# Experts four at a time in column tiles of 32 slots, with plain fp32 weights, and dilated sums on VectorE

## The reference

```
q = rms_norm_2(heads(q, DIL_DH), dil_q_norm_g[l, gi])
k = rms_norm_2(heads(k, DIL_DH), dil_k_norm_g[l, gi])
...
def hier_moe(h, w_rg, b_rg, w_re, b_re, w_gate, w_up, w_down):
    g_sel = jnp.argmax(g_logit, axis=-1)                 # one group of experts per token
    top_v, top_i = lax.top_k(e_logit, TOP_K)             # two experts in it
    gate = jax.nn.softmax(top_v, axis=-1) * g_p[:, None]
    ...
    def expert_block(args):
        xb, e = args
        return (jax.nn.silu(xb @ w_gate[e]) * (xb @ w_up[e])) @ w_down[e]
    ...
    out = jnp.zeros((T + 1, D), jnp.float32).at[row_t].add(yb.astype(jnp.float32) * row_w[:, None])[:T]
```

## Time and profile before

| | us |
|---|---|
| median of 3 runs | 3622.94 |
| lowest, highest | 3620.98, 3625.41 |
| the profiled execution | 3620.94 |
| its span (first to last instruction) | 3619.1 |
| experts' first product | 3025.05 |
| end of the experts' products | 3603.19 |

### The profile page before, as it was taken

How to read it: one execution, slowest core, us unless ns; L and a number is a source line. 1 busy time by engine, 2 the same in 40 slices (tenths; PEclk the granted TensorE clock), 3 DMA queues, 4 the chain that set the end, 5 groups by cost and what they waited for, 6 DMA issues and landing times. The chain is left out here.

```text
span 3619.1 us, 45453 instructions
## 1 busy us (share of the span) xinstructions
PE 3464.6 (96%) x17876; PEld 2860.6 (79%) x17876; DVE 2210.6 (61%) x3051; ACT 1413.9 (39%) x1566; POOL 413.2 (11%) x327
## 2 busy tenths in 40 slices
PE   7999999998999999999979999999998998999998
PEld 6888888755978887888749888977877877888886
DVE  7746547548755468567877333653226336999998
ACT  4211111447422232222335222433324225877876
POOL 2000000200110012000322000100000012333331
PEclk9999999999999999999989999999999998999999
DMA  6423323210244335444342222231222226999997
GB/s 252 136 84 117 104 91 105 74 50 1 94 137 142 110 112 180 146 160 154 97 123 76 93 94 85 73 133 59 82 93 70 88 90 240 364 362 361 366 377 296
DMA packets 321395, 531.12 MB, mean 147 GB/s; under 512 B 20564, under 2 KB 276609, under 8 KB 295360
## 3 DMA queue, kind: packets, MB, share of 16 engines
q1 hardware_dynamic: 307872, 512.46, 40.8%
q0 software_dynamic: 11040, 12.91, 1.1%
q10 hardware_dynamic: 2304, 3.24, 0.4%
HBM read 519.91 MB, written 25.17 MB: 151 GB/s over the span
## 5 line engine op out<-in xcount | busy, mean ns | idle before, releaser
L552 PE MATMUL banks<-operand_hi,trunk_weights_hi 128*128 128x512 f32 (+1 forms) x1568 | 566.8, 362 | 28.1 <-DVE trunk_weights_lo L1347 11.4
L552 PE MATMUL banks<-operand_lo,trunk_weights_hi 128*128 128x512 f32 (+1 forms) x1568 | 558.7, 356 | 0.0
L552 PE MATMUL banks<-operand_hi,trunk_weights_lo 128*128 128x512 f32 (+1 forms) x1568 | 558.5, 356 | 0.0
L552 PEld LDWEIGHTS banks<-operand_hi,trunk_weights_hi 128*128 128x128 f32 x1568 | 298.6, 190 | 78.7 <-DVE trunk_weights_lo L1347 13.1
L552 PEld LDWEIGHTS banks<-operand_lo,trunk_weights_hi 128*128 128x128 f32 x1568 | 298.8, 191 | 41.7
L552 PEld LDWEIGHTS banks<-operand_hi,trunk_weights_lo 128*128 128x128 f32 x1568 | 298.1, 190 | 42.1
L4390 DVE TENSOR_TENSOR ex_w_lo<-weight_ring,ex_w_hi 128x2048 fp32r<-128x2048 f32 x128 | 291.7, 2293 | 41.3 <-ACT ex_w_hi L4318 41.3
L1347 DVE TENSOR_TENSOR trunk_weights_lo<-weight_ring,trunk_weights_hi 128x2048 fp32r<-128x2048 f32 x90 | 206.0, 2288 | 163.1 <-ACT trunk_weights_hi L1302 163.1
L4318 ACT ACTIVATE ex_w_hi<-weight_ring 128x2048 fp32r<-128x2048 f32 x128 | 245.4, 1918 | 76.6 <-PE banks L4216 63.5
L1302 ACT ACTIVATE trunk_weights_hi<-weight_ring 128x2048 fp32r<-128x2048 f32 x90 | 171.7, 1908 | 215.8 <-PE banks L552 215.5
L552 PE MATMUL banks<-trunk_hidden_hi,trunk_weights_hi 128*128 128x512 f32 (+1 forms) x672 | 233.1, 347 | 4.1 <-DVE X L1373 1.7
(11 more groups left out here) (615 smaller groups left out, 7270.5 us busy)
## 6 DMA issues: line engine op xcount, KB each, us to landing
weight_ring<-ffn_w SPq DMA_DIRECT2D x120, 1024.0 KB, 4.9
weight_ring<-w_mod SPq DMA_DIRECT2D x72, 1024.0 KB, 4.9
weight_ring<-w_gate SPq DMA_DIRECT2D x64, 1024.0 KB, 7.4
weight_ring<-w_up SPq DMA_DIRECT2D x64, 1024.0 KB, 7.1
room<-w_down SPq DMA_DIRECT2D x64, 1024.0 KB, 7.1
weight_ring<-w_in SPq DMA_DIRECT2D x26, 1024.0 KB, 5.0
weight_ring<-ffn_w SPq DMA_DIRECT2D x16, 768.0 KB, 4.4
weight_ring<-o_w_pw SPq DMA_DIRECT2D x8, 1024.0 KB, 6.7
```

Source lines behind the costliest of these rows:

```text
L552: ins = pe.matmul(bank[:, at:at + width], w, x[:, at:at + width], start=start and n == 0, stop=stop and n == len(passes) - 1)
```

## The change

Three things change.

First, the experts are taken four at a time (a quad; the loop's step for one quad is a unit). The 128 columns of PE's array are four tiles of 32: tile j holds 32 slots of expert j of the quad, and `side_by_side` (L4424) issues for the four tiles a plain fp32 product each. There are three sets of 32 slots, so a round holds 96 slots of each expert. A unit has 6 phases (gate, up, down, two each); in each, four chunks, one of each expert, are used by all three sets. The weights are not split: PE reads the landed chunks. There are 16 places of 1 MB (2 + 4 + 8 + 2 in `expert_room`, the weight ring and `room`), and all of the first 16 chunks are loaded during `project_and_route`. The chunks of a phase are replaced when it is done (`load_after`): experts 0 and 1 of the quad by SP, 2 and 3 by ACT between its activations. The last unit's rows are multiplied by their gates, split into high and low, and brought to their tokens by fp32r products; the additions of the chosen rows are written beside the last phases.

Second, the router cuts the places into 18 blocks of 32 slots instead of 4 of 128, adds each expert's first lane, and has no entries for the last expert's gates.

Third, the squares of the dilated query heads are turned and summed in blocks of 32 by DVE (L3529, L3530), and one `fold` of four products (L3539) at the end of the stage adds the four blocks for all heads.

```diff
-            if dst is dil["q"]:
-                def pe_part(pe, bank, s):
-                    pe.wait_ge(s.act, s.acts_before(projected - 1))
-                    for t in range(ST):
-                        at = 512 + (g * GH + m) * ST + t
-                        ins = pe.matmul(k.PS[3][:, at:at + 1], sq(i)[:, t // 2, (t % 2) * P:(t % 2 + 1) * P], k.ones[:, 0:1], start=True, stop=True)
-                    return ins
+        def squares_summed(i, head):
+            def dve_part(dve, bank, s):
+                if head:
+                    dve.wait_ge(s.dve, s.dves_before(projected[i]) - 1)
+                for u in range(2):
+                    s.link(dve, dve.transpose(turned, sq(i)[:, u, :]))
+                    ins = dve.tensor_reduce(partial[:, head, 2 * u:2 * u + 2, :], turned.rearrange("p (t b c) -> p t b c", t=2, c=BLOCK), AXX, ALU.add)
...
+        def fold(pe, bank, s):
+            pe.wait_ge(s.dve, s.dves_before(queries[-1]))
+            for b in range(P // BLOCK):
+                ins = pe.matmul(k.PS[3][b * BLOCK:(b + 1) * BLOCK, 512:512 + GROUPS * GH * ST].rearrange("p (h t) -> p h t", t=ST),
+                                k.fold[:], partial[:, :, :, b], start=True, stop=True)
...
             def split_off(act, bank, s):
-                if i >= 2:
+                if i - 2 in summed:
                     act.wait_ge(s.out, summed[i - 2] + 1)
+                elif i >= 2:
+                    act.wait_ge(s.dve, s.dves_before(projected[i - 2]))
...
-CHUNKS = 6
+QUADS, QUAD, SETS, ROUNDS = EXPERTS // 4, 4, 3, 6
+PHASES, ROOM = 6, 16
+CHUNKS = PHASES * QUAD
...
-            sp.wait_ge(s_wlo, SLOTS + PIECES - 1)
-            for c in (*GATE, *UP):
-                load_expert_chunk(k, sp, c, 0, other=int(c in UP))
+            for c in range(2):
+                load_expert_chunk(k, sp, 0, c, 0)
+            for c in range(SLOTS):
+                sp.wait_ge(s_wlo, c + PIECES)
+                load_expert_chunk(k, sp, 0, 2 + c, 0)
+            sp.wait_ge(s_out, KD)
+            for c in range(6, 10):
+                load_expert_chunk(k, sp, 0, c, 0)
             for t in range(ST):
                 sp.wait_ge(s_ca, 2 * t + 2)
                 sp.dma_start(k.rows_dram[t * P:(t + 1) * P, :], HR[:, t, :]).then_inc(s_rows, 16)
+            for c in range(10, ROOM):
+                load_expert_chunk(k, sp, 0, c, 0)
...
+        def load_after(eng, p, u, f, which):
+            phase_done(eng, p, u, f)
+            for j in which:
+                if f < 2:
+                    load_expert_chunk(k, eng, u, QUAD * (f + 4) + j, 8 * (p % 4) + 4 * u)
...
-            def three(out, x, w, start, stop):
-                passes = ((x[0], w[0]), (x[0], w[1]), (x[1], w[0]))
-                for i, (a, b) in enumerate(passes):
-                    ins = pe.matmul(out, a, b, start=start and i == 0, stop=stop and i == 2)
-                return ins
+            def side_by_side(out, s, x, f, u, at, start, stop):
+                for j in range(QUAD):
+                    lanes = slice(BLOCK * j, BLOCK * (j + 1))
+                    ins = pe.matmul(out[lanes], x[:, lanes], raw[(CHUNKS * u + QUAD * f + j) % ROOM][:, at:at + 512], start=start, stop=stop)
+                return ins
+            def phase(f, s, p, u):
+                if s == 0:
+                    for j in range(QUAD):
+                        n = CHUNKS * u + QUAD * f + j
+                        pe.wait_ge(landed[n % ROOM], 48 * p + 16 * (n // ROOM + 1))
+                if f < 4:
+                    for i in range(4):
+                        kk = 4 * (f % 2) + i
+                        ins = side_by_side(G(s) if f < 2 else U(s), s, XT[:, s, kk, :], f, u, 512 * i, kk == 0, kk == KD - 1)
...
+            for i in range(6):
+                if i >= 2:
+                    pe.wait_ge(s_xc, i - 1)
+                turn_x(i, 0, 0)
             n = last_pair(pe)
-            with pe.Fori(0, n) as m:
-                step(m, 1)
-                step(m, 2)
+            with pe.Fori(0, n) as p:
+                unit(p, 0)
+                unit(p, 1)
+            unit(n, 0)
+            unit(n, 1, last=True)
```

More of the change, by code:

```diff
@@ L3533, in norm @@
         def norm(i, g, m, dst, gain, projected):
[L3536 to L3545 removed]
+            summed[i] = len(jobs)
             nth = len(scaled)
@@ L3783, in mixture @@
         XR = sb("x_rows", [P, ST, D])
-        gates, last_gates = sb("gates", [P, 2, ST]), sb("last_gates", [P, ST])
+        gates = sb("gates", [P, 2, ST])
         pairs = sb("pairs", [P, 1], I32)
[L3786 to L3790, removed]
@@ new lines, in mixture @@
+        room = sb("expert_room", [P, 10, SLOT])
+        base = k.weights.taken
+        k.raw = [room[:, c, :] for c in (8, 9)] + [k.weights.ring[:, (base + c) % SLOTS, :] for c in range(SLOTS)] + \
+            [room[:, c, :] for c in range(8)] + [to_rows(MX)[:, SLOT * c:SLOT * c + SLOT] for c in (0, 1)]
+        k.raw_landed = [k.sem(f"ex_raw_landed{c}") for c in range(ROOM)]
+        project_and_route(k, MX, XR, HR, operands, gates, pairs, ids, tokens)
+        experts(k, XR, HR, last_rows, pairs, ids, tokens, gates, out)
@@ L3815, in project_and_route @@
+def project_and_route(k, MX, XR, HR, operands, gates, pairs, ids, tokens):
     nc, a, W = k.nc, k.a, k.weights
@@ L4096, in _, with experts @@
                 pool.tensor_tensor(squares[:, 0, :], squares[:, 0, :], squares[:, m, :], ALU.add).then_inc(s_sum, 1)
-def experts(k, XR, XG, pairs, ids, tokens, gates, last_gates, out):
+def experts(k, XR, HR, last_rows, pairs, ids, tokens, gates, out):
     nc = k.nc
@@ L4151, in _ @@
+            with sp.Fori(0, n) as p:
+                loads(p, 0)
+                loads(p, 1)
+            loads(n, 0)
+            loads(n, 1, 2)
+            phase_done(sp, n, 1, 3)
             sp.wait_ge(s_landed, 1)
@@ L4448, in _, with unit @@
                     dve.scalar_tensor_tensor(XR[:, t, :], taken(t)[:, c, :], gates[:, c, t:t + 1], XR[:, t, :], ALU.mult, ALU.add).then_inc(done, 1)
+            def unit(p, u, last=False):
+                for s in range(SETS):
+                    hidden(s, p, u)
+                if not last:
+                    for i in range(6):
+                        x_out(i, p, u + 1)
+                    for s in range(SETS):
+                        rows_right(s, p, u)
+            for i in range(6):
+                x_out(i, 0, 0)
+            n = last_pair(dve)
+            with dve.Fori(0, n) as p:
+                unit(p, 0)
+                unit(p, 1)
+            unit(n, 0)
+            dve.tensor_copy(token_last[:], tokens[:, span(of(n, 1, SETS, 0), SETS)]).then_inc(s_token, 1)
+            unit(n, 1, last=True)
+            dve.wait_ge(s_lane, 1)
+            dve.wait_ge(s_token, 1)
+            for s in range(SETS):
+                dve.tensor_scalar(hot(s), lanes, token_last[:, s:s + 1], None, ALU.is_equal).then_inc(s_hot, 1)
+            add_chosen(0)
+            add_chosen(1)
+            rows_lo(0)
+            add_chosen(2)
+            rows_lo(1)
+            add_chosen(3)
+            rows_lo(2)
             for t in range(ST):
```

637 lines of the change are left out of this document (311 added, 326 removed).

## The result

| | before | after |
|---|---|---|
| median (us) | 3623.9 | 3592.22 |
| lowest, highest | 3620.98, 3625.41 | 3590.41, 3595.37 |
| the profiled execution | 3620.94 | 3590.91 |
| its span | 3619.1 | 3589.1 |
| experts' first product to the end of the last | 578.14 | 555.26 |

Four runs each give a ratio of 0.9914, with a 95% interval from 0.9897 to 0.9932: 31 us less, where 37 were forecast (3584). The change was in the forecast's direction and the time in its range (3566 to 3613); it lies 8 us above the point.

The account below looks back on a forecast made before the run. PE was taken to bound the expert stage. From 3620.94, the terms -37.3 (products), -10.1 (dilated sums), +2 and +2 (start), +6 (branches), +0.5 (router) and -0.4 (end) sum to -37.3, giving 3584 us; range 3566 to 3613.

Parts of the forecast that it names:

- The unit: Expert stage: four experts take 67.6 us where 71.2 stood; eight such take 540.8 against 578.1, so -37.3.
- half group of 0.429: Four records of the narrow fp32 products, 0.429 us apart at L1572; a group of eight records takes 0.858.
- the 1.5 for changes of form and set: Per four experts: 0.6 for six changes of form, 0.9 for 18 boundaries between phases and sets.
- Branches: PE's expert loop, whose body grows to 2448 records: three passes at 2 us each, +6, bounds 0 and 12.
- Dilated sums: Twelve query heads each lose a block of one-column products, -10.7; the new fold costs about 0.6; together -10.1.
- Start: Opening of the expert stage: +2 for three gathers and 24 transposes, and +2 for slow first products after idling.
- The second +2: Expert stage's first products run slow after PE idles about 10 us, as at L1572: +2, other end 0.
- Router: Loses four small DVE operations, gains a few on 18 blocks of slots instead of 4: +0.5, between 0 and +1.
- End: After the experts: 48 products for 16 double ones, additions moved under last phases, three new splits: -0.4, between -5 and +5.
- Rival A: Expert stage becomes bound by DMA, deciding below 366 GB/s; result 3600, at worst 3613; chance 0.18.
- Rival B: Expert stage: PE cannot keep up narrow products in one stream; at 63 ns a record 3661; chance 0.12.
- Rival C: Expert stage: a round holds 96 tokens an expert, so a second round is needed; +541, 4125; chance 0.02.

## Why the prediction was right, and where its size was off

The direction and the bound that were forecast were right: PE bounds the stage in both kernels, and the sum over PE's products gives it.

- **The unit**, 67.6 us: 67.45. The half group of 0.429 from the earlier trace rows held over 540 us; the 3 x 0.55 + 3 x 0.87 for transposes and the 1.5 for changes of form and set, 5.8 together, were 67.45 - 61.8 = 5.65. The stage without branches is 540.99 against 540.8.
- **Branches**, +6: +14.3. This is the step that was off, by 8.3 us, and by itself it moves the forecast of 3584 to 3592. It took three branches at 2 us: the 1.38 of the earlier trace rows, rounded up. There were two, since the last pass doesn't go back, at 6.56 and 7.72. The FFN's loop was the right neighbour for the mechanism, but the price was read from a place where the DMA engines are not full, and without the slow clock that follows 4.65 us of idle time. Both were to be had before: DMA share 0.97 in the earlier trace rows, and 2.2 us lost after an idle stretch in the earlier trace rows, which the prediction spent on the start alone. The slow clock even stood right behind the row that gave the price. The windows of PE in the kernel before (length, PE busy, clock, DMA share, GB/s), where PE idled for 1.23 and 1.38 us just before:

```profile
268.00:270.00 2.00, 0.78 (x4) 0.93 0.01 4
270.00:272.00 2.00, 2.00 (x7) 0.50 0.56 147
```

- **Dilated sums**, -10.1: -10.9 in the trace, -12.7 (8 to 17) alone. DVE's 24 transposes of 0.445 and 24 reductions of 0.420 are hidden; the fold took 0.3 instead of 0.6.
- **Start**, +2 and +2: +4.8, near in part by luck. Of it 2.0 are the gather (8.1 us from issue to the first transpose before, 10.1 after), 2.8 the 24 transposes through two banks with DVE's copies of 0.69 between (3.5 before, 6.3 after). The second +2, a slow clock over the first products, didn't come: their clock is 1.00 from 3018 to 3020, and the 0.53 from 3012 to 3015 lies over the transposes. The gather's 2.0 is about what it varies by (10.0 and 11.9 us in two executions of the changed kernel).
- **Router**, +0.5: +0.1. **End**, -0.4: -0.8.
- **Rival A** needed a limit under 366 GB/s; 423 were to be had. **Rival B** needed half groups over 0.46; they took 0.429. "TensorE: Matmul & The Clock Gate", Part 3, Measured speedup, of the Trainium skill has less than the full gain for tiles side by side. Four column tiles here give the full one: a group of four takes 0.858 us, and one plain fp32 product of the full 128 columns took 0.88 (L4304 of the kernel before: two records each, the first of 16 at 3604.0 and the last at 3610.6). **Rival C**: one round did.

The stations of unchanged code gave 1.6 us and took 1.2. The second of them, from the last dilated product to the router's logits, took from 286.1 to 289.8 us in kernels that are equal up to there, so such differences mean nothing.

## What to carry to other kernels

A loop of PE that goes back costs nothing as long as its body is held (912 and 1424 records here), and some microseconds per pass where it isn't (1936 and 2448). That price is to be taken from a place where the DMA engines are as busy as they will be at the branch, and the slow clock behind the idle time belongs to it. The branch's own record and the instruction packets in the DMA view show it directly. Where a change makes a loop's body larger, ask for the prefetch hint of the back edge or write the loop out; each took the whole 14.3 us out of the stage here. A transfer rate that a kernel shows while PE never waits is what it asked for, and need not be what it could get.

## What the runs showed of the hardware that was not expected

- The same taken branch of PE cost 1.4 to 1.7 us with no weight loads, 6.6 to 7.7 beside full DMA engines (some 4.6 of it idle, the rest at the lower clock), and nothing with the hint. Its record took 3.4 to 3.6, 6.7 and 0.5 us; the difference between the first two is the time before the target's packet starts.
- A body of 1424 records brought no instruction packet in 150 us of its passes; one of 1936 brought 10 of 16 KB in each pass.
- Where PE waited for its weights, loads of 1 MB each, DMA moved 422 to 424 GB/s in each of four stretches of 100 us (3050 to 3450) on this core.
- An indirect gather of 128 rows of 4 KB took 11.7 us from its issue, with the DMA engines at 14 to 31 GB/s for the first 9 of them.
